# Norm gains folded into the projection weights on chip, in a hybrid decoder layer on eight Trainium2 cores

## The reference

```python
h = rms_norm(x, pre_norm_g[layer])
proj = h @ w_in[layer]
a_u, a_v, sq, sk, sv, mq, z = jnp.split(proj, split_at, axis=-1)
y_a = chunked_spatial_gating(jax.nn.gelu(a_u), jax.nn.gelu(a_v), ...)
y_b = sliding_window_attention(sq..., sk..., sv..., attn_sinks[layer], rel_bias)
mkv = rms_norm(mem, mem_norm_g[layer]) @ w_mem_kv[layer]
mk, mv = jnp.split(mkv, 2, axis=-1)
y_c = memory_cross_attention(mq..., mk..., mv...)
y = jnp.concatenate([y_a, y_b, y_c], axis=-1) * jax.nn.silu(z)
x = x + rms_norm(y @ w_out[layer], post_norm_g[layer])
```

## Time and profile before

| | |
|---|---|
| median of two timed runs | 622.03 us (621.91 to 622.15) |
| the profiled execution | 620.88 us |
| its span on the slowest core, core 1 | 619.2 us |
| spans of the eight cores | 612.1 to 619.2 us |
| mean granted TensorE clock of the cores | 0.939 to 0.952 of full speed |
| DMA | 64.53 MB in all, 104 GB/s on the mean |

### The profile page before, as it was taken

How to read it: one execution, slowest core, us unless ns; L and a number is a source line. 1 busy time by engine, 2 the same in 40 slices (tenths; PEclk the granted TensorE clock), 3 DMA queues, 4 the chain that set the end, 5 groups by cost and what they waited for, 6 DMA issues and landing times.

```text
span 619.2 us, 11372 instructions; the slowest of 8 cores (612.1 to 619.2 us)
## 1 busy us (share of the span) xinstructions
PE 536.8 (87%) x3428; PEld 269.9 (44%) x3428; DVE 378.1 (61%) x1010; ACT 308.7 (50%) x558; POOL 159.9 (26%) x284
## 2 busy tenths in 40 slices
PE   0581896899899989998999899998999899998973
PEld 0351543454355434544445435543445444543431
DVE  0521473467666785668475765678476767476494
ACT  2312254654764366535755456526753575447521
POOL 5302220214031331134121412143112413142141
PEclk9995796899899989997999979997999999999997
DMA  8999991110333312330333332330333211122145
GB/s 183 205 192 222 227 147 38 68 70 2 103 103 103 102 57 80 129 116 31 103 103 103 104 102 92 114 103 2 101 104 119 88 69 68 70 69 69 69 167 174
DMA packets 25551, 64.53 MB, mean 104 GB/s; under 512 B 3473, under 2 KB 11793, under 8 KB 25490
## 3 DMA queue, kind: packets, MB, share of 16 engines
q1 hardware_dynamic: 16130, 54.88, 26.9%
q0 software_dynamic: 9360, 8.91, 10.8%
HBM read 55.92 MB, written 16.78 MB: 117 GB/s over the span
## 4 chain that ended last, share of the span: by engine, by line
PE 66%; DMA 9%; DVE 9%; issue 7%; ACT 5%; POOL 2%; SPq 1%; DVEq 0%; ACTq 0%; POOLq 0%
PE bk L462 33%; PE bk L733 14%; PE bk L520 7%; DMA sb_F<-mem 3%; DMA sb_F<-wsT 2%; DMA sb_F<-ident 2%; PE bk L487 2%; PE bk L400 2%; DVE sb_F L756 2%; DVE sb_hT L403 1%; PE bk L684 1%; DVE sb_E L590 1%; DMA out<-sb_F 1%; ACT sb_Em L613 1%; PE bk L580 1%
## 5 line engine op out<-in xcount | busy, mean ns | idle before, releaser
L462 PE MATMUL bk<-sb_hT,sb_win_bf 128*128 128x512 bf16 x1088 | 254.5, 395 | 3.1 <-DVE sb_hT L403 2.8
L462 PEld LDWEIGHTS bk<-sb_hT,sb_win_bf 128*128 128x128 bf16 x1088 | 108.0, 101 | 141.3 <-issue 27.0
L733 PE MATMUL bk<-sb_wout_bf,sb_yT 128*128 128x512 bf16 x512 | 118.3, 383 | 11.4 <-ACT sb_Em L613 6.7
L739 DVE TENSOR_TENSOR sb_F<-bk,sb_gpost 128x512 f32<-128x512 f32 x64 | 43.2, 688 | 63.7 <-ACT sb_junk L736 63.5
L733 PEld LDWEIGHTS bk<-sb_wout_bf,sb_yT 128*128 128x128 bf16 x512 | 48.2, 98 | 67.8 <-issue 17.1
L742 POOL TENSOR_SCALAR sb_r<-sb_ss 128x1 f32<-128x1 f32 x32 | 11.0, 343 | 254.7 <-ACT sb_junk L736 254.7
L390 DVE TENSOR_SCALAR sb_xs<-sb_F,sb_rrA 128x1024 bf16<-128x1024 f32 x36 | 41.6, 1158 | 45.7 <-POOL sb_rrA L383 45.6
L736 ACT ACTIVATE sb_junk<-bk 128x512 bf16<-128x512 f32 x64 | 38.9, 607 | 59.9 <-PE bk L733 58.5
L379 ACT ACTIVATE sb_xs<-sb_F 128x1024 bf16<-128x1024 f32 x36 | 37.9, 1052 | 38.7 <-DMA sb_F<-mem 23.2
L588 ACT ACTIVATE sb_E<-bk 128x512 f32<-128x512 f32 (+1 forms) x64 | 35.6, 582 | 43.1 <-DVE sb_den L668 25.6
L520 PE MATMUL bk<-sb_win_bf,sb_hT 128*128 128x512 bf16 x256 | 56.5, 379 | 0.0
(11 more groups left out here) (79 smaller groups left out, 625.9 us busy)
## 6 DMA issues: line engine op xcount, KB each, us to landing
sb_F<-x SPq DMA_DIRECT2D x64, 512.0 KB, 4.0
out<-sb_F SPq DMA_DIRECT2D x32, 512.0 KB, 2.9
sb_win_bf<-win POOLq DMA_DIRECT2D x4, 1024.0 KB, 54.9
sb_F<-mem SPq DMA_DIRECT2D x4, 512.0 KB, 12.5
sb_wout_bf<-wout POOLq DMA_DIRECT2D x2, 1024.0 KB, 32.3
sb_win_bf<-win POOLq DMA_DIRECT2D x1, 1280.0 KB, 21.8
sb_wmem_bf<-wmem POOLq DMA_DIRECT2D x1, 1024.0 KB, 35.7
sb_EBT<-ebias SPq DMA_DIRECT2D x1, 512.0 KB, 13.0
```

What stands on the lines that cost most here:

```text
L462: r = q.matmul(out=bk[:], lhsT=win_bf[:, k, col:col + P], rhs=hT.t[sb][:, k, :], start=(k == 0), stop=(k == 7))
L733: r = q.matmul(out=bk[:], lhsT=yT.t[yi][:, k, :], rhs=wout_bf[:, k, hs], start=(k == 0), stop=(k == 7))
L739: op("dve", lambda q: q.tensor_tensor(out=tOt[:, hs], in0=bk[:], in1=gpost[:, hs], op=ALU.mult), reads=[gpost_b], writes=[tO_b[half]], exc ...
```

## The change

The gain of both norms moves from the transposed activations to the weights. The instruction at L403 becomes a plain copy (L422 in the changed kernel); it no longer reads `gpre` or `gmem`. A branch that would put the copy on ACT is there too, but the list that chooses holds "dve" and nothing sets it otherwise. In exchange each piece of `W_in` and the memory weights are multiplied in place after they are loaded: eight DVE instructions for a piece, one for each group of 128 rows (L345, L351), 56 in all. The matmuls that read a piece now wait for its eight instructions. The two loads of `wout_bf` are issued earlier, straight behind the last piece of `W_in`.

```diff
--- before.py
+++ after.py
@@ -339,6 +339,19 @@
         op("pool", lambda q: q.dma_start(out=win_bf[:, :, c0:c1], in_=win_v[:, :, c0:c1]),
            writes=[win_b[k][j] for k in range(8)], dma_key=f"W{j}")
 
+    def scale_win_piece(j):
+        c0, c1 = PIECES[j]
+        for k in range(8):
+            op("dve", lambda q, k=k: q.tensor_scalar(out=win_bf[:, k, c0:c1], in0=win_bf[:, k, c0:c1],
+                                                     scalar1=gpre[:, k:k + 1], scalar2=None, op0=ALU.mult),
+               reads=[gpre_b, win_b[k][j]], writes=[win_b[k][j]])
+
+    def scale_wmem():
+        for k in range(8):
+            op("dve", lambda q, k=k: q.tensor_scalar(out=wmem_bf[:, k, :], in0=wmem_bf[:, k, :],
+                                                     scalar1=gmem[:, k:k + 1], scalar2=None, op0=ALU.mult),
+               reads=[gmem_b, wmem_b[k]], writes=[wmem_b[k]])
+
     def load_wmem():
         op("pool", lambda q: q.dma_start(out=wmem_bf[:], in_=wmem_v), writes=wmem_b, dma_key="Wm")
 
@@ -390,6 +403,8 @@
         op("dve", lambda q: q.tensor_scalar(out=xs.t[j][:], in0=ft[:], scalar1=rrA.t[j][:, 0:1], scalar2=None,
                                             op0=ALU.mult), reads=[fb, rrA.b[j]], writes=[xs.b[j]])
 
+    EVAC_ENG = ["dve"]
+
     def A_tr(j, gam, gam_b, dst_t, dst_col, dst_buf):
         bk, bkb = nb()
         bkv = bk[:].bitcast(BF16).rearrange("p (k c) -> p k c", k=8)
@@ -400,9 +415,12 @@
                 r = q.transpose(out=bkv[:, k, :], in_=xs.t[j][:, k * P:(k + 1) * P], identity=ident_bf[:])
             return r
         op("pe", tr, reads=[xs.b[j], ident_bf_b], excl=[bkb])
-        op("dve", lambda q: q.tensor_tensor(out=dst_t[:, :, dst_col:dst_col + P], in0=bkv,
-                                            in1=gam[:].unsqueeze(2).to_broadcast([P, 8, P]), op=ALU.mult),
-           reads=[gam_b], writes=[dst_buf], excl=[bkb])
+        if EVAC_ENG[0] == "act":
+            op("act", lambda q: q.activation(out=dst_t[:, :, dst_col:dst_col + P], in_=bkv, func=AF.Copy),
+               writes=[dst_buf], excl=[bkb])
+        else:
+            op("dve", lambda q: q.tensor_copy(out=dst_t[:, :, dst_col:dst_col + P], in_=bkv),
+               writes=[dst_buf], excl=[bkb])
 
     def stageA(src_ap, gam, gam_b, dst_t, dst_col, dst_buf):
         i = A_load(src_ap)
@@ -803,13 +821,16 @@
     A_t(3)
     load_win_piece(4)
     load_win_piece(5)
+    load_wout()
     mem_pre(0)
     setup_rest()
+    scale_win_piece(0)
+    scale_win_piece(1)
     stageB_part(0, 0)
     mem_tr(0)
     mem_pre(1)
+    scale_wmem()
     mem_kv(0)
-    load_wout()
     A_ld(4)
     mem_tr(1)
     A_ld(5)
@@ -819,6 +840,8 @@
     A_pr(5)
     A_pr2(5)
     mem_kv(1)
+    scale_win_piece(2)
+    scale_win_piece(3)
     stageB_part(0, 1)
     setup_ebt()
     A_t(4)
@@ -853,6 +876,10 @@
             A_pr2(q + 8)
         if 0 <= q - 2 < NT:
             D_fin(q - 2)
+        if q == -2:
+            scale_win_piece(4)
+        if q == -1:
+            scale_win_piece(5)
         if 0 <= q + 4 < NT:
             stageB_part((q + 4) // 4, (q + 4) % 4)
         if q == -2:
```

## The result

| | before | changed |
|---|---|---|
| median of the timed runs | 622.03 us | 643.55 us |
| lowest | 619.82 us | 641.93 us |
| the profiled execution | 620.88 us | 644.38 us |
| median of the eight cores' spans | 616.0 us | 638.8 us |
| v projection of superblock 0 starts, median of the cores | 68.3 | 79.5 |

The ratio is 1.0345, 95% interval 1.0324 to 1.0367: slower by 21.5 us on the medians. The ratio leaves out three runs in which one die was slowed down, while the medians are over all 10 and 11 runs and would hardly differ without them. The last three rows are read from the timelines of all eight cores, each core's own start and span. They split the program in two: a start in which the change costs 29.7 us, and a rest in which it gives back 7.4. On core 1 alone, whose rows follow, the start costs 23.9 (133.1 to 157.0).

The account below looks back on a forecast made before the run. PE, busy 87%, was taken as the bound, with DVE time counting only where PE waits. Start +30.1 less 2.7 gave +27.4 on 620.88, so 648.3; with the median's offset 649, rounded down to 648.5, range 639 to 657.

Parts of the forecast that it names:

- The start: Up to the end of the second half of z: late scaled weights delay PE, running total +30.1 us.
- the v projection: Superblock 0: waits for pieces 2 and 3, scaled behind memory block 1's casts; starts at 80.3, 10.4 later.
- the last block of z: Second half of z: 32 matmuls wait for piece 5 until 117.6, take 9.6; +8.2, total +30.1.
- the first memory product: First block's key/value product: waits for scaled memory weights until 62.8, takes 6.2 us on a slow PE, ends 69.0.
- The first half of z: Waits for piece 4, scaled behind the attention exponentials' products; mask product done at 106.9, not 98.14: +8.8, total +21.9.
- One scaling: DVE product of 512 bf16 columns: 0.30 us each, 2.4 us for eight, bounds 0.26 and 0.42.
- Slow clock behind each stand: After PE stands in the start, the next 32 matmuls take 9.58 or 9.6 us instead of 7.07.
- The W_out load at zero: POOL's queue: loads issued behind the last W_in piece cost zero, if the queue takes them at once.
- POOL's queue would be full: Rival: early W_out issue holds POOL and block 0's pows; held until 50, the time is 657; chance 5%.
- 5 x 0.55 = 2.7 us: Steady part: the shorter copy takes 0.55 us off each of PE's five waits, 2.7 of 10.3 us.
- rival 2: Steady part: the copy closes the five waits ahead of L684, giving back 23 us: 628; 5% together with another rival.
- a sign for it: Prediction wrong if the distance from the second z half to the end shrinks by much more than 3 us.

Follow-up runs that it names:

- m1: Changed kernel with the eight products of the memory weights put ahead of memory block 1's loads and xs products: 638.79 us, ratio 1.0285.
- m2: Changed kernel with the memory weights and piece 2 scaled ahead of memory block 1, piece 3 directly behind mem_tr(1): 629.79 us, ratio 1.0125.
- m3: Changed kernel with memory weights and pieces 0, 2, 3, 4 and 5 scaled where DVE waits, all 56 products made: 613.45 us, ratio 0.9882.
- e3_tiny: Changed kernel with each of the 56 scaling instructions cut to two columns, places and waits kept: 635.32 us, ratio 1.0234.
- e5_fill: Changed kernel with 18, 40 and 30 idle matmuls on PE ahead of the waits for pieces 2 and 3, 4 and 5: 636.26 us, ratio 1.0248.
- e4_wout_early: Kernel before with only the two W_out loads issued right behind the last W_in piece: 619.91 us, ratio 0.9993.
- e6: Kernel before with the copy in place of the product only for the six tiles whose evacuation PE waits for at L684: 614.30 us, ratio 0.9892.
- e7: Kernel before with the copy for all tiles from 8 on except the six PE waits for at L684: 620.97 us, ratio 1.0010.
- e2: Changed kernel with the product at L403 put back, so the gain is applied twice: 647.49 us, ratio 1.0437.
- e1_copy_only: Kernel before with the plain copy in place of the product at L403 and nothing else: 610.72 us, ratio 0.9841.
- m4_all_fill: Changed kernel with scalings where DVE waits, plus idle matmuls on PE, 40 ahead of memory block 1 and 12 ahead of piece 4: 612.69 us, ratio 0.9872.

## Why the prediction came out right

The time forecast was 648.5 with 639 to 657; 643.55 was measured, and slower by over 2% held.

- *The start.* Forecast +30.1, measured +29.7 on the median of the cores. On those medians the steps fit too: the v projection 11.2 later for a forecast 10.4, L317 22.1 for 21.9, the last block of z 28.5 for 29.1. On core 1, from whose rows the sum was made, all steps but the first memory product came early and the start cost only 23.9, so that the closeness of the total is in part luck. The steps on core 1: first projection at 34.5 (34.49 measured), the first key/value product at 62.8 (63.25), the second at 71.2 (70.22), the v projection at 80.3 (78.76). The first half of z was put 13.1 + 2.4 - 1.1 behind 93.8, at 108.2 or so (106.00), L317 at 120 (117.30), the last block from 139.5 (134.09 on core 1; 134.09 to 140.79 over the cores). What makes core 1 early at the end is the stretch from L317 until PE stands ahead of the last block, taken over at 12.3 us: cores 1 and 7 ran the bias at the fast pace and took 9.9, the other six took over 12.
- *That order decides*, and not transfers or work, is shown by m1, m2 and m3, which move nothing but places and take the start from 160.9 to 128.8. e3_tiny points the same way: with half of the scalings' DVE time gone, 14.5 of the 21.5 us stay.
- *One scaling* was put at 0.30 and measured 0.27: 1 us too much over 40. (The 0.33 that bounded it from above sets the spacing of L500, 0.26, beside the duration of the xs product, 0.75; two durations give 0.40.) Of the two rates weighed, the one of four elements a cycle, which the Trainium skill gives (VectorE: DVE Perf Modes, the perf-mode tier table), is the nearer one in this trace: an instruction of 512 columns takes 346 ns, above the 0.29 us that the prediction estimated from it but below the 422 of L550, and from 2 to 512 columns the time grows by 121 ns.
- *The copy*: 0.67 forecast, 0.687 measured.
- *Slow clock behind each stand*: the sum put 9.6 or so for each of the three blocks, and they took 9.19, 9.22 and 8.84 on core 1 and up to 9.88 elsewhere; e5_fill takes 6.0 off by this alone. The first memory product was put at 6.2 and took 5.0, from 63.25 to 68.24.
- *The W_out load at zero*: e4_wout_early shows it. That POOL's queue would be full was a rival and didn't occur: on core 1 both loads are issued by 24.6, and the power for block 0 runs at 28.16.
- *The mis-sized term* is "5 x 0.55 = 2.7 us" for the steady part. The rest gave back 7.4, and the copy alone 6.6. Each wait shrank by the half microsecond forecast (10.3 to 7.4 for the five). e6 and e7 show that nearly all of the gain in the rest comes with these waits (5.8 of the 6.6), and the block timings say that the larger part is the clock behind them. The slow blocks behind these waits stood in the prediction as part of a rival and at nothing in the sum. It is rival 2 in small: the waits didn't close, as that rival asked, but shortening them by a quarter already recovered part of the 2.5 us behind each. This is why the result lies 5 below the forecast. The prediction named a sign for it: the distance from the second half of z to the end was not to shrink by much more than 3 us, and it shrank by 6.0 on the median of the cores.

Left open: why the start of the changed kernel is 3.3 later than e2's, and whether the copy's 2.4 in the start alone is more than the 1.5 by which e4's start differs with nothing gained.

## What to carry to other kernels

In a program whose engines run their lists in order, the price of added set-up work can lie in where it stands: 15 us of DVE work cost 27 us behind the wrong waits (e2_scale_only) and 2.5 in stretches in which DVE waited (m3_all beside e1_copy_only). Before placing such work, list what each engine waits for in the start and when each input lands, and put each piece directly behind its input's arrival and ahead of the next long wait. Look for the evacuations that TensorE waits for: here six of 36 carried 5.8 of the 6.6 us gained in the steady part, and eighteen others nothing.

## What was not expected of the hardware

- With half a microsecond taken off waits of 1.9 to 2.4 us, the 32 matmuls of 512 columns behind each took 8.06 us on the mean (e6_copy_t1) where they took 8.83 before; at a granted clock of 1.00 they take 7.07.
- A two-column tensor_scalar lasts 225 ns, and 0.14 us each in a row; a 512-column one of bf16 346 ns and 0.27. So half of the price of the larger one stays when its columns go.
- Idle matmuls ahead of a wait took 6 us off in e5_fill. In m4_all_fill 52 of them moved the total by nothing that shows, though the two blocks behind them ran at 7.07 and 7.23.
